# Latent attention: the loads of the fifth and sixth head stand ahead of a modulation weights' load on SyncE's queue

## The reference

```
sh1, sc1, g1, sh2, sc2, g2 = split(silu(c) @ w_mod + b_mod, 6)      # w_mod is 1024 x 6144
h_lat, h_ctx = modulate(x, sh1, sc1), modulate(ctx, csh1, csc1)
q, k, v (8 latent heads of 96/96/64), qs, ks, vs (windowed heads) = project(h)
mix = concat(softmax(q k^T * scale) v over all 1280 keys,  windowed attention with a sink logit)
x = x + g1 * (mix @ w_out)
x = x + g2 * (relu(modulate(x, sh2, sc2) @ w_mlp1)^2 @ w_mlp2)
```

## Time and profile before

| what | us |
|---|---|
| median of 3 runs | 1397.72 (1397.13 to 1399.58) |
| the profiled execution: its own time / span of its trace | 1399.78 / 1398.0 |
| busy: PE, PE weight load, DVE, ACT, POOL | 1357.5, 1149.4, 914.6, 692.6, 487.1 |
| latent attention in the trace | about 359 to 634 |

### The profile page before, as it was taken

One profiled execution on the slowest core, in us unless ns is written; L12 is line 12 of the kernel. 1 busy time (PEld: TensorE's weight loads), 2 busy tenths in 40 slices (PEclk: granted clock), 3 DMA queues, 4 the chain that ended last, 5 costly groups with the idle time before them and its releaser, 6 DMA issues.

```text
span 1398.0 us, 18825 instructions
## 1 busy us (share of the span) xinstructions
PE 1357.5 (97%) x7262; PEld 1149.4 (82%) x7262; DVE 914.6 (65%) x1284; ACT 692.6 (50%) x1343; POOL 487.1 (35%) x321
## 2 busy tenths in 40 slices
PE   5899997999999999999999999999999999999999
PEld 1688987999899988988887888888888888888887
DVE  1878776777777877875774646547564654746463
ACT  2755655788778777972223424333332433333240
POOL 2766553121299992501102303132050323205010
PEclk8999998999999999999999999999999999999999
DMA  9555658433365646301123112121211212121013
GB/s 377 192 162 160 177 159 286 129 89 86 115 199 144 190 131 191 71 1 61 31 76 121 31 31 90 31 75 31 62 44 30 91 31 75 30 62 44 15 61 121
DMA packets 121576, 143.42 MB, mean 103 GB/s; under 512 B 8184, under 2 KB 103288, under 8 KB 118672
## 3 DMA queue, kind: packets, MB, share of 16 engines
q1 hardware_dynamic: 121232, 142.18, 32.6%
q0 software_dynamic: 256, 0.05, 0.0%
HBM read 108.38 MB, written 31.74 MB: 100 GB/s over the span
## 4 chain that ended last, share of the span: by engine, by line
PE 70%; DVE 11%; POOL 7%; ACT 6%; DMA 4%; issue 1%; SPq 1%; DVEq 0%; ACTq 0%; POOLq 0%
PE f_ps L2062 24%; PE f_ps L2331 19%; PE o_ps L1770 6%; PE a_ps L1422 4%; PE a_ps L1438 3%; PE f_ps L2347 3%; POOL l_wg L1349 3%; ACT s_pr L1519 3%; POOL l_gate L1351 3%; PE t_ps L956 2%; PE a_ps L1468 2%; DVE s_nmx L1604 2%; PE t_ps L945 1%; DMA t_wm<-in_w_mod 1%; DMA l_v<-scratch_v 1%
## 5 line engine op out<-in xcount | busy, mean ns | idle before, releaser
L2062 PE MATMUL f_ps<-h,f_w 128*128 128x512 f32 x1536 | 358.0, 389 | 0.4 <-DVE h L1836 0.2
L2062 PEld LDWEIGHTS f_ps<-h,f_w 128*128 128x128 f32 x1536 | 288.1, 188 | 60.7 <-DVE h L1836 0.7
L2261 DVE TENSOR_TENSOR mix<-mix,f_ps 128x512 f32<-128x512 f32 x196 | 128.7, 683 | 152.9 <-PE f_ps L2331 152.9
L2102 POOL TENSOR_TENSOR f_w<-f_w,f_g 128x1024 f32<-128x1024 f32 x30 | 77.0, 2590 | 390.2 <-DMA f_w<-in_w_mlp 342.7
L2139 ACT ACTIVATE f_a<-f_ps 128x512 f32<-128x512 f32 x64 | 38.2, 597 | 254.7 <-PE f_ps L2062 254.7
L2331 PE MATMUL f_ps<-f_bh,f_al 128*128 128x512 f32 x392 | 152.5, 389 | 0.0
L2331 PE MATMUL f_ps<-f_bh,f_ah 128*128 128x512 f32 x392 | 152.5, 389 | 0.0
L2331 PE MATMUL f_ps<-f_bl,f_ah 128*128 128x512 f32 x392 | 152.5, 389 | 0.0
L1618 DVE TENSOR_TENSOR l_pT<-a_ps,l_pT 128x512 fp32r<-128x512 f32 (+1 forms) x192 | 108.9, 594 | 54.0 <-ACT l_pT L1529 53.9
L1422 PE MATMUL a_ps<-l_k,l_q 96*128 96x512 f32 (+1 forms) x576 | 136.5, 366 | 1.6 <-DMA l_v<-scratch_v 1.1
L956 PE MATMUL t_ps<-w_in,t_h 128*128 128x416 f32 (+2 forms) x600 | 125.7, 355 | 0.3 <-DVE w_in L719 0.3
(11 more groups left out here) (223 smaller groups left out, 2425.1 us busy)
## 6 DMA issues: line engine op xcount, KB each, us to landing
l_wg<-in_w_mod SPq DMA_DIRECT2D x8, 2048.0 KB, 8.0
f_w1r<-in_w_mlp SPq DMA_DIRECT2D x32, 512.0 KB, 4.0
f_w<-in_w_mlp SPq DMA_DIRECT2D x16, 1024.0 KB, 5.0
t_wm<-in_w_mod SPq DMA_DIRECT2D x8, 1024.0 KB, 12.5
scratch_k<-t_kT SPq DMA_DIRECT2D x20, 384.0 KB, 3.7
l_k<-scratch_k SPq DMA_DIRECT2D x8, 960.0 KB, 10.6
scratch_q<-t_qT SPq DMA_DIRECT2D x16, 384.0 KB, 3.9
l_q<-scratch_q SPq DMA_DIRECT2D x8, 768.0 KB, 6.3
```

The costliest lines, as they stand in the source:

```text
L2062: last = nc.tensor.matmul(ps[:, b, :], w1[:, g % 2, w, k, :], h2[x][:, k, half * HB:(half + 1) * HB], start=(k == 0 and i == 0), stop=(k = ...
L2261: V.tensor_tensor(x, x, ps[:, bank_of(i, t), :].rearrange("p (k c) -> p k c", c=P), ALU.add).then_inc(added, 1)
```

## The change

SP's program issues the same transfers in another order. Before: load(2), gate chunks 3 and 4, load(3), chunks 5 and 6, load(4), chunk 7, load(5), `w_out`. After: load(2), chunks 3 and 4, load(3), chunk 5, load(4), chunk 6, load(5), chunk 7, `w_out`. No other engine's program differs, and no transfer is added or taken away.

```diff
         for h in range(2, HEADS):
             sp.wait_ge(out_ready, NU + HEAD_U * (h - 1))
             load(h)
-            if h < 4:
-                load_gate(2 * h - 1)
-                load_gate(2 * h)
-            if h == 4:
-                load_gate(KC - 1)
+            if h == 2:
+                load_gate(3)
+                load_gate(4)
+            if 2 < h < 6:
+                load_gate(h + 2)
             if h == 5:
                 sp.wait_ge(wg_used, KC)
                 for k in range(KC):
```

## The result

The changed kernel is slower: 1406.12 us median (1404.05 to 1407.29, 6 runs) against 1398.51 us for the kernel before in the same comparison, ratio 1.0053, 95% interval 1.0040 to 1.0066. The forecast was slower, 1401.9 us, with a range to 1404.6 us; the measured time lies above the range. Of 7.6 us lost I had forecast 4.2 us.

What follows compares the result with a forecast made beforehand. PE, busy 97% of the span, was taken to bound the kernel. ACT's later path gave +4.2 us, with -1.4 us from load(4) contained, added to the 1397.72 us median: 1401.9 us, range 1396.6 to 1404.6 us.

Steps and rivals of the forecast that it cites:

- Terms 1 to 3: Latent attention: load(4) wait gone, -1.4 us; chunk 7 late for GpSimd, 7 us; PE waits 0.9 us at gate's sum.
- term 4: `w_out` goes out 7.0 us later, load(6) and ACT's first rounding are late behind it; result +4.2 us.
- term 1: PE at head 4: the wait for load(4) goes, -1.4 us.
- PE can make up 0.4 us: +4.2 us: Head 6: ACT's first rounding of `w_out` starts 4.6 us later, PE makes up 0.4 us, leaving +4.2 us.
- the pipeline restarts badly: Rival, behind PE's wait: ACT's backlog or a falling granted clock costs 3.5 to 7 us; 1405 to 1409 us; chance 0.07.
- the chunk did not arrive early: Denies the rival that chunk 7 lands by 513.9 us, leaving only the -1.4 us gain: 1396.3 us; chance 0.10.
- the two waits were not shorter: Denies the rival of shorter waits at gate's sum and head 6: +0.5 to +2.7 us, 1398.2 to 1400.4 us; chance 0.20.
- load(4) was not late: Denies the rival that load(4) can't go out earlier or lands late nevertheless: 1403.3 us; chance 0.03.
- the first rival: Load(5) and chunk 7 overlap in the queue, so the chunk lands by 513.9 us: 1396.3 us; chance 0.10.

Runs made afterwards that it cites:

- ten matmuls: The changed kernel with 10 extra matmuls on PE just ahead of its wait for load(6); 1403.84 us, ratio 1.0032.
- ten matmuls and ACT early: The changed kernel with 10 extra matmuls ahead of PE's wait for load(6) and ACT's wait for the gate's stores before its sixth rounding; 1401.90 us, ratio 1.0018.
- 16 matmuls: The changed kernel with 16 extra matmuls on old operands just ahead of PE's wait for load(6); 1403.65 us, ratio 1.0029.

## Why the prediction was wrong

The steps, each against what was measured in the changed kernel's first profile:

| step | forecast, us | measured, us |
|---|---|---|
| load(4) issued; PE's idle at 490 | 469.4; none | 469.19; none |
| load(5) issued, chunk 7 issued | 502.0, 503.7 | 501.90, 503.60 |
| chunk 7 landed | 519.5 (511.3 to 520.3) | 519.8 |
| GpSimd's idle; gate done | 7; 539.2 | 7.59; 539.54 |
| PE's wait at the gate's sum | 0.9 | 1.32 |
| `w_out` issued | 539.26 | 539.57 |
| load(6) landed; PE's wait | 563.3; 3.5 | 564.0; 3.70 |
| ACT's first rounding | 562.8 | 563.30 |
| first scores of step W+49, 564.45 in the kernel before | 568.7 (564.45 + 4.2) | 572.01 |

Terms 1 to 3 hold, and term 4 up to its last step. That load(4) alone is a gain is shown by the kernel with it alone (-1.14 us in the stretch, ratio 0.9987, where term 1 has -1.4 us); that the late chunk makes all of the loss, by the one with chunk 7 alone. That the loss passes through load(6) and the stores behind `w_out`, by the kernel that takes load(6) out from behind it, whose time is that of the kernel before.

The step that failed is the closing of term 4: "PE can make up 0.4 us: +4.2 us". It took the work behind the wait at the durations of before. In place of that, PE worked behind the wait at half its clock, for 6.8 us in one profile and 3.4 us in the other. Without that, late load(6) at +2.97 us and ACT at +1.12 us make +4.09 us, nearly what I had forecast. The first profile has 7.72 - 4.09 = 3.63 us on top of it, but not all of this is the clock's: there load(6) also landed later. From the issue of load(3) to the first scores of head 6 it is 560.27 - 436.98 = 123.29 us before and 564.05 - 436.72 = 127.33 us in the first profile, +4.04 us, against +2.97 us in the second (561.11 - 434.85), +3.11 us with ten matmuls (563.38 - 436.98) and +3.06 us with ten matmuls and ACT early (562.76 - 436.41). Behind those first scores 3.68 us were lost in the first profile and 2.27 us in the second, against 0.98 us with ten matmuls and nothing with ACT early as well. So the clock's part is about 2.7 us in the first profile, where the low stretch was 6.8 us, and 1.3 us in the second, where it was 3.4 us; by the medians, filling the wait with 16 matmuls gave back 2.7 us. Filling it left load(6) and ACT as late as they were and took the low clock away, which shows the cause.

I had this as a rival, "the pipeline restarts badly", priced at 3.5 to 7 us and with a chance of 0.07. The argument against it, that the wait leaves PE busy for 0.87 of its slice, was bad: it looks at a mean over 35 us, in which an idle of 3.7 us vanishes. The trace of the kernel before had the answer in finer rows. In the token phase PE's timeline shows an idle of the same kind:

```profile
229.23 1.51 PE L945 MATMUL t_ps<-ident,t_sn 128*128 128x128 f32 x6 [3.67 <-DVE t_sn L781]
```

and the windows around it, where the clock is the third number from the end:

```profile
225.00:229.00 4.00, 0.56 (x3) 0.13 (x1) 3.21 (x9) 1.75 (x5) 1.74 (x2) 0.97 1.00 365
229.00:231.00 2.00, 1.60 (x7) 1.26 (x7) 2.00 (x7) 0.63 (x2) 0.90 (x2) 0.50 1.05 374
231.00:233.00 2.00, 2.00 (x10) 2.00 (x10) 1.84 (x4) 0.94 (x2) 1.92 (x4) 0.50 1.14 359
233.00:235.00 2.00, 2.00 (x11) 1.94 (x11) 1.72 (x3) 0.69 (x2) 0.04 (x1) 0.50 1.09 380
235.00:237.00 2.00, 1.99 (x15) 1.75 (x14) 1.82 (x4) 1.97 (x4) 0.00 (x0) 0.86 1.06 380
```

That is 6.8 us at 0.50, from the last half us of an idle of 3.67 us on. Whoever had read these rows would have put up to 3.4 us behind my wait of 3.5 us and come to 1405.3 us at most. The idle of 1.15 us that load(4) caused in the kernel before had no such tail, but it is a third as long as the wait that was forecast.

The other rivals: the chunk did not arrive early, as it landed 16.2 us after its issue, behind the whole of load(5), as chunk 3 and load(2) had let me expect; the two waits were not shorter but a little longer (1.32 and 3.70 us against 0.9 and 3.5 us); and load(4) was not late. One reading in the first rival was off: chunk 7 was expected 1.7 us behind the issue of its load and chunk 3 was 9.7 us behind, so it was issued 8 us earlier relative to its load, not 10 us. That changed nothing.

What stays open: why the stretch at 0.50 was 3.4 us in two of the four profiles that have it at head 6 and 6.8 us in the other two. The length of the idle (2.32 and 2.54 us against 2.55 and 3.70 us) does not settle it. The idle of 3.67 us in the token phase stands in all eleven profiles of this case, at the same place and of the same length; it was followed by 3.4 us at 0.50 in four of them and by 6.8 us in seven. A shorter one, some 11 us behind it and 2.88 us long in most profiles, is even followed by none in four of them, as in that of the kernel with chunk 7 late, where the clock is 1.00 from 237 to 248 us:

```profile
241.75 1.09 PE L1441 MATMUL a_ps<-ident,s_pr 128*128 128x128 f32 x8 [2.88 <-DVE t_qT L747]
```

So an idle of one length in one place can be priced only within a range, here from nothing to 6.8 us at the lower level. And what part of the spread of the changed kernel's runs (1402.9 to 1407.7 us over both comparisons) the low stretch makes was not measured run by run.

## What to carry to other kernels

A transfer moved ahead in an in-order queue pushes another back: ask of the one pushed back who waits for it last, and of that one what stands behind it in the same queue. Here 4 us of lateness in a place with a price of 1.4 us were bought with 7 us in a place that three others hung on; the half of the move that touched only the chunk with slack was the gain. And a wait that is new to PE has a second price, the time at which PE works behind it: look in the traces, in windows of 2 us, for what the clock did behind an idle of that length, and in more than one execution.

## What was not expected of the hardware

At head 6 an idle of PE between 2.32 and 3.70 us was followed by 3.4 or 6.8 us at the lower level in each of four profiles, beginning between 0.3 us before PE's restart and 1.9 us behind it (in the token phase up to 1.3 us before it). Idles of 0.3 to 1.7 us (the waits for load(4) before and at the gate's sum, and the rests of the filled waits) were followed by none, and the one of 2.88 us some 11 us behind that of the token phase by none in four of the eleven profiles. The Trainium skill ("TensorE: Matmul & The Clock Gate", HAM oscillation) describes just this, matmul bursts that restart at half rate behind a wait for a DMA; the traces agree in kind.

Four stores of 4 KB each, issued behind a large load, were as late as the load: in the changed kernel their issue alone held SP for 11.11 us, and they landed at 563.2 us, 0.8 us ahead of load(6). With load(6) and `w_out` in the other order SP needed 2.86 us for them.
